# A mixture-of-experts layer step: gathered rows on three of every four partitions, half of the down product in f16 halves, SwiGLU clamps on the activation engine, weights split two units at once

## The chip, the cores and the metric

The kernel runs on one core of a Trainium2 chip. The metric is device time in microseconds (us) of one execution. Before the change the median of three runs is 1374.02 us (1372.73 to 1379.13). Five engines work side by side, each through its own list of instructions in order: TensorE (PE, with its weight loads PEld), VectorE (DVE), ScalarE (ACT), GpSimd (POOL) and SyncE (SP, which here only issues transfers). They wait for each other by semaphores alone. Sixteen DMA engines move data between the device memory, SBUF (128 partitions) and the tensors there.

## The reference

One inference step of a one-layer streaming encoder over 512 prompt rows and 64 sample rows of width 1024, all in f32:

```python
proj = x @ w_in -> [u | q | k | v | r | gate code]
A = multi-scale causal pooling mixer on u;  B = gated linear attention on q, k, v
h = LN1(alpha * x + concat(A, B) @ w_out)
y = LN2(alpha * h + MoE(h))            # and new pool and attention states

# MoE: top 4 of 32 experts by softmax router; each expert on its own rows xb
gu = xb @ w_gu[e] + b_gu[e]                              # 1024 -> 2 x 1024
gate, up = gu[:, :1024], gu[:, 1024:]
gate = minimum(gate, 7.0);  up = clip(up, -7.0, 7.0)
hmid = gate * sigmoid(1.702 * gate) * (up + 1.0)
out = hmid @ w_down[e] + b_down[e]                       # 1024 -> 1024
y_row = sum over the row's 4 experts of softmax weight * out
```

Each expert has 12 MB of f32 weights, 32 experts 403 MB. An expert has 72 rows on average.

## The kernel before, in words

The stage before the experts (projections, pooling, attention, first norm, router) takes about the first 285 us and is hardly touched. Then 32 experts follow, each in a block of 96 row places; experts with more rows get further blocks in a loop behind the 32, which the inputs of these runs do not enter.

**Weights.** SP loads an expert in six pieces of 2 MB (four of `w_gu`, two of `w_down`) into a ring of eight slots of 4096 f32 per partition. It may load a piece once the piece that held the slot has been read: for `w_gu` once DVE has split it (semaphore `split_done`), for `w_down` once PE has read it (`down_read`).

**Split products.** The product with `w_gu` runs in f16 halves. A *unit* is a block of 128 output columns with its 8 blocks of the inner dimension: 128x1024 elements. ACT writes the high half `whi = f16(1024 w)` (`hi`, L782), DVE then the low half `wlo = f16(1024 w - whi)` (`lo`, L1531). An expert has 16 units: 0 to 3 gate and 4 to 7 up of the first half of the hidden vector, 8 to 15 the same of the second half. There are 8 buffers for split units, so a unit can be split only when PE has used the unit eight before (`unit_used`). Per unit PE runs 24 matmuls of 96 columns (`unit`, L854).

**Activation.** Per half, DVE adds the bias, clamps and multiplies in seven instructions of 128x384 (`act_half`, L1501 to L1516), with the sigmoid on ACT between (L787). The result `hm` is the hidden vector, in f32.

**Down product.** PE multiplies `hm` by `w_down` in f32 straight from the ring (`down`): 16 products of 96x512, each of which is shown as two matmuls.

**Rows.** POOL gathers the rows of an expert two experts ahead with an indirect DMA into `xg`, 96 partitions (L582); the places come from a small product of one-hot `hot` with `info` (`table`, `rows_of`). PE transposes them (`rows`, L1098), ACT and DVE split them (`rows_hi` L774, `rows_lo` L1522). The output is weighed by ACT (L796) and scattered by POOL (L595).

**Order.** The order on every engine is written out by hand in its block. DVE, per expert: one-hot, lo of units 8 to 13, `act_half` 0, `rows_of`, lo 14 and 15, `act_half` 1, `rows_lo`, lo of units 0 to 7 of the next expert. PE: units 0 to 7, table, units 8 to 15, transposes of the next rows, down. At the end the partial rows of the four top-k places are loaded (L463), added on DVE (L1612) and on PE, and normed.

## Time and profile before

| | us |
|---|---|
| median of three runs | 1374.02 |
| lowest, highest | 1372.73, 1379.13 |
| profiled execution, own time | 1378.18 |
| its span (first to last instruction) | 1376.4 |
| PE busy | 1294.2 (94%) |
| DVE busy | 1009.2 (73%) |
| ACT busy | 677.4 (49%) |
| mean granted TensorE clock | 0.974 of full speed |

A profile shows one execution. Busy times of engines overlap; a share is an average over stages with different limits. "idle before" in a row is the time the engine stood still ahead of the instruction, and behind the arrow stands what ended it. The mean duration of one matmul is longer than its distance to the next, because matmuls are pipelined. Slices are fortieths of the span, 34.4 us each. The line numbers are of the kernel before.

### The profile page before, as it was taken

To read this page: it belongs to the slowest core of one execution; us is meant where nothing else is said; L and a number is where in the kernel's file an instruction comes from. 1 tells how busy PE (TensorE), PEld (TensorE's weight loads), DVE (VectorE), ACT (ScalarE), POOL (GpSimd) and SP (SyncE) were. 2 spreads that over 40 slices of the span, in tenths; PEclk is the share of its full clock that TensorE was granted. 3 is DMA by queue.
4 is the path that set the end of the run, shared out by engine and by line. 5 is a ranking of instruction groups with operands and counts; after the bars stand their busy time and mean duration, and the time that the engine had idled before them with its cause. 6 is when DMAs were issued, how large, how long until landed. Compare 5 with 4: busy or idle time off the path is not lost.

```text
span 1376.4 us, 34739 instructions
## 1 busy us (share of the span) xinstructions
PE 1294.2 (94%) x15208; PEld 885.9 (64%) x15208; DVE 1009.2 (73%) x1576; ACT 677.4 (49%) x814; POOL 121.9 (9%) x139
## 2 busy tenths in 40 slices
PE   6999989948999999999999999999999999999995
PEld 3446644446777777666666777777766666777652
DVE  4542436458888888788878788888878778787877
ACT  4531221044555655566655666555556556565611
POOL 1000811010100000000000000000000000000002
PEclk9999999959999999999999999999999999999997
DMA  9540155087999999999999999999999999999993
GB/s 323 210 181 1 55 192 214 16 315 281 398 401 409 413 411 412 414 413 409 400 407 414 410 412 409 412 414 414 417 409 404 407 411 410 410 413 414 390 389 101
DMA packets 50007, 472.62 MB, mean 343 GB/s; under 512 B 8542, under 2 KB 9333, under 8 KB 24637
## 3 DMA queue, kind: packets, MB, share of 16 engines
q1 hardware_dynamic: 38860, 436.22, 78.0%
q0 software_dynamic: 10336, 31.77, 6.4%
q8 instruction: 122, 2.00, 0.6%
q10 hardware_dynamic: 656, 2.36, 0.5%
q14 instruction: 33, 0.26, 0.1%
HBM read 446.43 MB, written 29.95 MB: 346 GB/s over the span
## 4 chain that ended last, share of the span: by engine, by line
PE 62%; DMA 10%; DVE 5%; issue 2%; ACT 1%; DVEq 0%; POOLq 0%
PE wide L854 45%; PE bank L854 16%; DMA ring<-in_w_gu 7%; DMA work<-part_rows 2%; DVE work L1531 2%; PE bank L1098 2%; ACT work L782 1%; DMA work<-h_rows,work 1%; DVE ring L1639 0%; DVE ring L1637 0%; DVE ring L1626 0%; DVE work L1501 0%; DVE work L1457 0%; DVE work L1504 0%; DVE ring L1373 0%
## 5 line engine op out<-in xcount | busy, mean ns | idle before, releaser
L1531 DVE SCALAR_TENSOR_TENSOR work<-ring,work 128x1024 f16<-128x1024 f32 x512 | 591.4, 1219 | 126.7 <-ACT work L782 126.3
L854 PE MATMUL wide<-ring,work 128*96 128x512 f32 (+4 forms) x1400 | 567.6, 564 | 1.8 <-ACT work L719 1.0
L782 ACT ACTIVATE work<-ring 128x1024 f16<-128x1024 f32 x512 | 500.8, 1048 | 80.6 <-DMA ring<-in_w_gu 68.2
L854 PEld LDWEIGHTS wide<-ring,work 128*96 128x96 f32 (+4 forms) x1400 | 215.2, 156 | 323.6 <-issue 299.1
L854 PE MATMUL wide<-work 128*128 128x96 f16 (+1 forms) x6262 | 304.5, 211 | 26.3 <-DVE work L1531 9.2
L854 PEld LDWEIGHTS bank<-work 128*128 128x128 f16 (+4 forms) x6450 | 296.0, 101 | 35.4 <-issue 23.4
L854 PE MATMUL bank<-work 128*128 128x96 f16 (+4 forms) x6450 | 301.8, 209 | 10.2 <-ACT work L755 3.8
L854 PEld LDWEIGHTS wide<-work 128*128 128x128 f16 (+1 forms) x6262 | 279.8, 99 | 46.6 <-issue 21.2
L787 ACT ACTIVATE work<-work 128x384 f32<-128x384 f32 x64 | 33.5, 524 | 199.8 <-DVE work L1504 199.8
L796 ACT ACTIVATE work<-wide,work 96x1024 f32<-96x1024 f32 x30 | 33.2, 1107 | 115.8 <-PE wide L854 115.7
L582 POOL DMA_INDIRECT work<-h_rows,work x32 | 31.8, 995 | 502.8 <-PE bank L1098 476.3
L595 POOL DMA_INDIRECT part_rows<-work x30 | 28.1, 938 | 426.2 <-ACT work L796 426.2
L774 ACT ACTIVATE work<-bank 128x384 f16<-128x384 f32 x64 | 28.2, 488 | 45.9 <-PE bank L1098 45.6
L1506 DVE SCALAR_TENSOR_TENSOR work<-wide,work 128x384 f32<-128x384 f32 x32 | 17.8, 557 | 41.5 <-PE wide L854 41.5
L1098 PE MATMUL bank<-work 96*128 96x96 f32 x256 | 28.5, 256 | 12.6 <-DMA work<-h_rows,work 12.1
L1522 DVE SCALAR_TENSOR_TENSOR work<-bank,work 128x384 f16<-128x384 f32 x64 | 32.6, 550 | 9.6 <-ACT work L774 9.5
L1416 DVE SCALAR_TENSOR_TENSOR ring<-ring,wide 128x1024 f32<-128x1024 f32 (+1 forms) x5 | 6.1, 1219 | 44.7 <-PE wide L854 44.7
L854 PE MATMUL wide<-work,ring 128*128 128x512 f16 (+2 forms) x296 | 38.7, 289 | 0.0
L1516 DVE TENSOR_TENSOR work<-work 128x384 f32<-128x384 f32 x64 | 35.9, 561 | 2.2
L1513 DVE SCALAR_TENSOR_TENSOR work<-work 128x384 f32<-128x384 f32 x64 | 35.8, 559 | 2.2
L1245 DVE SCALAR_TENSOR_TENSOR ring<-ring 128x1024 f16<-128x1024 f32 x16 | 19.0, 1222 | 20.4 <-ACT ring L670 20.4
L1098 PEld LDWEIGHTS bank<-work 96*128 96x128 f32 x256 | 23.7, 146 | 12.8 <-DMA work<-h_rows,work 12.2
(191 smaller groups left out, 609.8 us busy)
## 6 DMA issues: line engine op xcount, KB each, us to landing
ring<-in_w_gu SPq DMA_DIRECT2D x128, 2048.0 KB
ring<-in_w_down SPq DMA_DIRECT2D x64, 2048.0 KB
part_rows<-work POOLq DMA_DIRECT2D x1, 10240.0 KB, 37.1
ring<-in_w_in SPq DMA_DIRECT2D x4, 2048.0 KB
ring<-part_rows SPq DMA_DIRECT2D x3, 2560.0 KB, 26.3
ring<-in_w_out SPq DMA_DIRECT2D x2, 2048.0 KB
h_rows<-work POOLq DMA_DIRECT2D x1, 2560.0 KB, 9.9
ring<-h_rows SPq DMA_DIRECT2D x1, 2560.0 KB, 20.9
```

Of the source, the lines that this page charges most:

```text
L582: pool.indirect_dma_start(xg, None, h_dram, bass.IndirectOffsetOnAxis(ap=tok_i[q], axis=0), bounds_check=PLACES - 1, oob_is_err=False)\
L595: pool.indirect_dma_start(part_dram, bass.IndirectOffsetOnAxis(ap=dst_i[p], axis=0), orow, None, bounds_check=TOPK * SPAN - 1, oob_is_err= ...
L774: act.activation(xhi[q][:, 4 * b:4 * b + 4, :], bank[b][:, 0:4 * BLK] .rearrange("p (k s) -> p k s", k=4), ACT.Copy, scale=X_UP).then_inc( ...
L782: act.activation(whi[u % BUFS], packed(s, u), ACT.Copy, scale=W_UP).then_inc(hi_done, 1)
L787: act.activation(sg, g1, ACT.Sigmoid, scale=SWISH).then_inc(sig_done, 1)
L796: act.activation(orow, wide[1 if isinstance(n, int) else 0][0:BLK, :], ACT.Copy, scale=slots[p][:, 5:6])\
L854: return pe.matmul(out, w, x, start=start, stop=stop, skip_group_check=True)
L1098: last = pe.transpose(bank[b][:, k * BLK:(k + 1) * BLK], xg[:, (4 * b + k) * P:(4 * b + k + 1) * P], ident[0:BLK, 0:BLK])
L1513: dve.scalar_tensor_tensor(u1, u1, 1.0, g1, ALU.add, ALU.mult).then_inc(gate_up, 1)
L1516: dve.tensor_tensor(hm[:, 4 * half:4 * half + 4, :], u1, sg, ALU.mult).then_inc(hm_done, 1)
L1522: dve.scalar_tensor_tensor(xlo[q][:, 4 * b:4 * b + 4, :], bank[b][:, 0:4 * BLK] .rearrange("p (k s) -> p k s", k=4), X_UP, xhi[q][:, 4 * b ...
L1531: dve.scalar_tensor_tensor(wlo[u % BUFS], packed(s, u), W_UP, whi[u % BUFS], ALU.mult, ALU.subtract).then_inc(split_done, 1)
```

## The change

Five edits:

1. The one-hot has 128 columns instead of 96. Places 3, 7, 11, ... stay empty (`iota16`, which DVE fills in about a dozen small steps ahead of the first one-hot, is -1 there), so the 96 places lie on three of every four of 128 partitions, and `xg` has 128 partitions. The transpose multiplies by `used`, a permutation that brings the 96 used partitions to the front. A small product with `used16` (`sel_ready`) brings destinations and weights into the same order, and `places_of` reads them.
2. ACT and DVE split two units at once: 128x2048 elements in 4 buffers instead of 128x1024 in 8.
3. The first four of the eight inner blocks of the down product run in f16 halves: the first `w_down` piece is split as two more pairs (10 an expert, not 8), the hidden half too (`hidden_hi` on ACT, `hidden_lo` on DVE).
4. The clamps become Relu on ACT: `from_limit` writes relu(7 - (g + b)), scaled, once per 96 columns, since its bias is per output column: four instructions a quarter. A second Relu bounds `up` from the other side. DVE keeps two instructions per half, `gated_half` and `hidden`.
5. Nine matmuls that compute nothing stand ahead of the first rows (`idle`), the load of the second expert's first piece waits for the first gather, and the one-hots of the last stage are made after the last expert's units.

```diff
-BUFS = 8
+BUFS = 4
+PAIRS = 10
@@ SP, per expert
-                    if i < 2:
-                        sp.wait_ge(down_read, e * 2 + (i + 1))
+                    if e == 0:
...
+                    elif i == 1:
+                        sp.wait_ge(down_read, e + 1)
                     else:
-                        sp.wait_ge(split_done, e * 16 + 4 * (i - 1))
+                        sp.wait_ge(split_done, PAIRS * e - 2 if i == 0 else PAIRS * e + 2 * i - 4)
+                    if e == 1 and i == 0:
+                        sp.wait_ge(gathered[0], 16)
@@ SP, last stage
-                    sp.wait_ge(split_done, 16 * E + (4, 12, 16)[j])
+                    sp.wait_ge(split_done, PAIRS * E + (0, 4, 6)[j])
                 else:
-                    sp.wait_ge(unit_used, unit_done(E - 1, 15))
+                    sp.wait_ge(unit_used, pair_done(E - 1, 8))
@@ ACT
+            def hi(n, p, s, got):
+                if p % 2 == 0:
+                    act.wait_ge(slot_in[s], got)
+                act.wait_ge(unit_used, pair_done(n, p) - BUFS)
+                act.activation(whi[buf(n, p)], packed(s, p), ACT.Copy, scale=W_UP).then_inc(hi_done, 1)
+            def from_limit(dst, b, at):
+                for c in range(4):
+                    last = act.activation(dst[:, c, :], b[:, c * BLK:(c + 1) * BLK], ACT.Relu, scale=-DOWN * S_UP,
+                                          bias=bguT[:, at[0], at[1] + c:at[1] + c + 1])
+                return last
+            def gate(n, half, e):
+                act.wait_ge(unit_used, pair_done(n, 4 * half + 1))
+                act.wait_ge(hm_done, n * 2 + (half + 2))
+                from_limit(g1, bank[2] if half == 0 else wide[0][:, 0:512], (e, 4 * half)).then_inc(gate_free, 1)
+                act.wait_ge(gate_free, n * 2 + (half + 3))
+                act.activation(sg, g1, ACT.Sigmoid, scale=-SWISH / S_UP, bias=sig_bias).then_inc(sig_done, 1)
+            def up(n, half, e):
...
+                act.activation(u1, u1, ACT.Relu, scale=-1.0, bias=up_bias).then_inc(up_clip, 1)
+            def hidden_hi(n):
+                act.wait_ge(hm_done, n * 2 + 3)
+                act.wait_ge(unit_used, pair_done(n - 1, 9))
+                act.activation(hh, hm[:, 0:4, :], ACT.Copy, scale=1.0 / S_UP).then_inc(hh_done, 1)
             for n in range(E):
-                for u in range(BUFS, 16):
-                    if u == 14:
-                        swish(n, 0)
-                    hi(n, u, piece_slot(n, u // 4), landed(n, u // 4))
-                swish(n, 1)
+                next_hi(n, 4)
+                next_hi(n, 5)
+                gate(n, 0, n)
+                next_hi(n, 6)
+                next_hi(n, 7)
+                up(n, 0, n)
+                next_hi(n, 8)
+                hidden_hi(n)
+                next_hi(n, 9)
+                gate(n, 1, n)
+                if n + 1 < E:
+                    next_hi(n + 1, 0)
+                    next_hi(n + 1, 1)
+                up(n, 1, n)
...
@@ PE
-                    for k in range(4):
-                        last = pe.transpose(bank[b][:, k * BLK:(k + 1) * BLK],
-                                            xg[:, (4 * b + k) * P:(4 * b + k + 1) * P],
-                                            ident[0:BLK, 0:BLK])
+                        last = pe.transpose(bank[b][:, k * BLK:k * BLK + P],
+                                            xg[:, (4 * b + k) * P:(4 * b + k + 1) * P], used)
@@ def down(n, s, got)
+                    pe.wait_ge(hl_done, n + 1)
+                    for k in range(4):
+                        pe.wait_ge(split_done, pairs(n) + (8 + k // 2 + 1 + 2 * BUFS))
...
+                        for x, w in ((hh, wh), (hh, wl), (hl, wh)):
+                            for c in range(2):
+                                last = mm(out[:, c * 512:(c + 1) * 512], x[:, k, :], w[:, c * 512:(c + 1) * 512],
+                                          k == 0 and x is hh and w is wh, False)
+                        if k % 2:
+                            last.then_inc(unit_used, 1)
+                first = 4 if isinstance(n, int) else 0
+                for k in range(first, KT):
                     if k % 4 == 0:
                         pe.wait_ge(hm_done, n * 2 + (k // 4 + 3))
+            def idle(count):
+                for _ in range(count):
+                    mm(wide[1][:, 512:1024], ident, oT[:, 0, 0:512], True, True)
+            idle(3)
             table(0, 0)
+            idle(6)
             rows(0, 0, 16, 1)
@@ DVE
+            step(dve.memset(iota16, -1.0))
...
+            def gated_half(n, half):
+                dve.wait_ge(sig_done, n * 2 + (half + 1))
+                dve.scalar_tensor_tensor(g1, g1, -LIMIT * S_UP, sg, ALU.add, ALU.mult).then_inc(gated, 1)
+            def hidden(n, half):
+                dve.wait_ge(gated, n * 2 + (half + 1))
+                dve.wait_ge(up_clip, n * 2 + (half + 1))
...
+                dve.scalar_tensor_tensor(hm[:, 4 * half:4 * half + 4, :], u1, (1.0 - LIMIT) * S_UP, g1, ALU.add, ALU.mult)\
+                   .then_inc(hm_done, 1)
+            def lo(n, p, s):
+                dve.wait_ge(hi_done, pairs(n) + (p + 1))
+                dve.wait_ge(unit_used, pair_done(n, p) - BUFS)
+                dve.scalar_tensor_tensor(wlo[buf(n, p)], packed(s, p), W_UP, whi[buf(n, p)],
                                          ALU.mult, ALU.subtract).then_inc(split_done, 1)
```

How the order on DVE moves shows best in its list. Before, from the last two splits of an expert on (L1531 is a lo, L1501 to L1516 are `act_half` 1, L1522 is `rows_lo`, L1457 the one-hot):

```order
L1531 SCALAR_TENSOR_TENSOR work<-ring,work 128x1024 x2
L1501 SCALAR_TENSOR_TENSOR work<-wide,work 128x384
L1504 TENSOR_SCALAR work<-work 128x384
L1506 SCALAR_TENSOR_TENSOR work<-wide,work 128x384
L1509 TENSOR_SCALAR work<-work 128x384
L1513 SCALAR_TENSOR_TENSOR work<-work 128x384
L1516 TENSOR_TENSOR work<-work 128x384
L1522 SCALAR_TENSOR_TENSOR work<-bank,work 128x384 x2
L1531 SCALAR_TENSOR_TENSOR work<-ring,work 128x1024 x8
```

After, from the pair 8 split on (L1623 is a lo of a pair, L1608 `hidden_lo`, L1594 `gated_half` 1, L1603 `hidden` 1, L1614 `rows_lo`):

```order
L1623 SCALAR_TENSOR_TENSOR work<-ring,work 128x2048
L1608 SCALAR_TENSOR_TENSOR work<-work 128x384
L1623 SCALAR_TENSOR_TENSOR work<-ring,work 128x2048
L1594 SCALAR_TENSOR_TENSOR work<-work 128x384
L1623 SCALAR_TENSOR_TENSOR work<-ring,work 128x2048 x2
L1603 SCALAR_TENSOR_TENSOR work<-work 128x384
L1614 SCALAR_TENSOR_TENSOR work<-bank,work 128x384 x2
```

Two splits of the next expert now stand between `gated_half` 1 and `hidden` 1; before, every split of the next expert stood behind the finished hidden vector.

On PE, one expert before (L1098 are the transposes):

```order
L854 MATMUL bank<-work 128x96 x192
L854 MATMUL bank<-work 96x4 x5
L854 MATMUL wide<-work 128x96 x192
L1098 MATMUL bank<-work 128x96 x8
L854 MATMUL wide<-ring,work 96x512 x16
```

and after:

```order
L918 MATMUL bank<-work 128x96 x192
L918 MATMUL bank<-work 128x4 x5
L918 MATMUL wide<-work 128x96 x192
L918 MATMUL bank<-work 96x4
L1167 MATMUL bank<-work 128x128 x8
L918 MATMUL wide<-work 96x512 x24
L918 MATMUL wide<-ring,work 96x512 x8
```

Eight of the sixteen f32 products of the down product became 24 f16 ones, ahead of the eight that stay f32; those eight wait for `hidden` 1.

## Rows read from the trace of the kernel before

**Rows 1.** The page's 40 slices: busy share of the DMA engines in tenths.
```profile
DMA  9540155087999999999999999999999999999993
```
**Rows 2.** Chain of waits: start us, us, engine, line, count; expert starts and down products.
```profile
342.80 3.40 PE bank L854 x72
...
456.56 13.73 PE wide L854 x32
...
629.93 8.43 PE bank L854 x197
...
1058.63 13.75 PE wide L854 x32
...
1286.61 13.74 PE wide L854 x32
1300.35 8.16 PE bank L854 x192
```
**Rows 3.** Waits of ACT for weights, first in 456:1058, then in 1060:1290.
```profile
ACT work L782 <- DMA ring<-in_w_gu: 13.5, 9, 2.9
...
ACT work L782 <- DMA ring<-in_w_gu: 50.0, 20, 5.1
```
**Rows 4.** Windows: us, busy of PE, PEld, DVE, ACT, POOL, PEclk, DMA share, GB/s.
```profile
622.00:624.00 2.00, 2.00 (x6) 0.81 (x5) 2.00 (x3) 2.00 (x3) 0.00 (x0) 1.00 1.03 326
...
634.00:636.00 2.00, 2.00 (x52) 2.00 (x49) 2.00 (x3) 2.00 (x3) 0.00 (x0) 1.00 1.03 434
```
**Rows 5.** Timeline of one expert, 616:650.
```profile
617.04 0.96 POOL L582 DMA_INDIRECT work<-h_rows,work  x1 [15.92 <-PE bank L1098]
...
618.54 9.16 DVE L1531 SCALAR_TENSOR_TENSOR work<-ring,work 128x1024 f16<-128x1024 f32 x8
...
633.35 3.90 ACT L782 ACTIVATE work<-ring 128x1024 f16<-128x1024 f32 x4 [0.28 <-PE bank L854]
...
647.19 0.84 PE L1098 MATMUL bank<-work 96*128 96x96 f32 x8
```
**Rows 6.** Groups by line and form: busy us, mean ns of one, idle before.
```profile
L782 ACT ACTIVATE work<-ring 128x1024 f16<-128x1024 f32 x512 | 500.8, 1048 | 80.6 <-DMA ring<-in_w_gu 68.2 <-PE bank L854 12.2
L787 ACT ACTIVATE work<-work 128x384 f32<-128x384 f32 x64 | 33.5, 524 | 199.8 <-DVE work L1504 199.8
...
L719 ACT ACTIVATE work<-bank,work 128x64 f32<-128x64 f32 x4 | 1.2, 306 | 0.0
...
L1531 DVE SCALAR_TENSOR_TENSOR work<-ring,work 128x1024 f16<-128x1024 f32 x512 | 591.4, 1219 | 126.7 <-ACT work L782 126.3
...
L1513 DVE SCALAR_TENSOR_TENSOR work<-work 128x384 f32<-128x384 f32 x64 | 35.8, 559 | 2.2
```
**Rows 7.** Timelines: gaps of PE late in the stage; then a window of its clock.
```profile
1120.97 3.81 PE L854 MATMUL wide<-work 128*128 128x96 f16 x48 [2.12 <-DVE work L1531]
...
1283.60 2.33 PE L854 MATMUL wide<-work 128*128 128x96 f16 x48 [1.68 <-DVE work L1531]
...
1122.00:1123.00 1.00, 1.00 (x16) 0.50 1.00 426
```
**Rows 8.** Timeline of the first expert's start.
```profile
287.78 1.54 POOL L582 DMA_INDIRECT work<-h_rows,work  x1 [5.32 <-DVE work L1470]
...
298.60 1.54 PE L1098 MATMUL bank<-work 96*128 96x96 f32 x8 [12.10 <-DMA work<-h_rows,work]
...
324.42 2.98 PE L854 MATMUL wide<-work 128*128 128x96 f16 x48 [3.37 <-DVE work L1531]
```
**Rows 9.** Timeline of the last stage, 1320:1352.
```profile
1336.57 4.49 PE L854 MATMUL bank<-work 128*116 128x512 f16 x20
1340.90 5.49 DVE L1612 TENSOR_TENSOR ring<-ring 116x5120 f32<-116x5120 f32 x1 [0.64 <-DMA ring<-part_rows]
1346.94 17.22 PE L854 MATMUL wide<-work 116*116 116x512 f32 x44 [5.89 <-DMA work<-part_rows]
...
1350.81 1.23 DVE L1626 SCALAR_TENSOR_TENSOR ring<-wide,ring 116x1024 f32<-116x1024 f32 x1 [4.41 <-PE wide L854]
```

More of the change, by code:

```diff
@@ L230, in build @@
         val_one = take(E * (MAXB - 1))
+        hot30 = half_at(cursor[0], PLACES)
+        take(PLACES // 2)
+        hh, hl = [h[:, 0:4 * BLK].rearrange("p (k s) -> p k s", k=4) for h in (hot30, hot31)]
+        used16 = half_at(A + PLACES + 528 + D, BLK)
+        assert PLACES + 528 + D + BLK // 2 <= 2304
+        sig_bias, up_bias = small[:, 88:89], small[:, 89:90]
         g2n, b2n = ring[:, 0:D], ring[:, D:2 * D]
@@ L1455, in onehot @@
                     place = rank[0:n, t, bass.ds(e, 1)] if first is None else small[0:n, 59 + t:60 + t]
-                    order = places_b if isinstance(m, int) and m % 2 else iota16
-                    last = dve.tensor_scalar(hot[0:n, t, :], order[0:n, :], place, 1.0 / W_UP,
-                                             ALU.is_equal, ALU.mult)
+                    last = dve.tensor_scalar(hot[0:n, t, :], iota16[0:n, :], place, None, ALU.is_equal)
                 last.then_inc(hot_ready, 1)
@@ L1565, in _ @@
                     dve.memset(gatesT, 0.0).then_inc(gatesT_zero, 1)
[L1566 to L1572 removed]
+                next_lo(n, 8)
+                hidden_lo(n)
+                next_lo(n, 9)
+                gated_half(n, 1)
+                if n + 1 < E:
+                    next_lo(n + 1, 0)
+                    next_lo(n + 1, 1)
+                hidden(n, 1)
                 if n + 1 < E:
                     rows_lo(n + 1, (n + 1) % 2)
[L1575 to L1576 removed]
+                    places_of(n + 1, (n + 1) % ROW_BUFS)
+                    next_lo(n + 1, 2)
+                    next_lo(n + 1, 3)
+            dve.wait_ge(unit_used, pair_done(E - 1, 9))
+            dve.wait_ge(tok_known, 1)
+            end_hot(0)
+            end_hot(1)
             dve.wait_ge(gates_hi, 1)
@@ L1604, in _ @@
                     rows_lo(b + E, 0)
-                    for u in range(16):
-                        if u == 14:
-                            act_half(b + E, 0, e)
-                        lo(b + E, u, u // 4)
-                    act_half(b + E, 1, e)
+                    places_of(b + E, 0)
+                    dve.tensor_copy(bguT[:, E, :], bguT[:, bass.ds(e, 1), :].rearrange("p a f -> p (a f)"))\
+                       .then_inc(ov_bias, 1)
+                    for p in range(6):
+                        lo(b + E, p, p // 2)
+                    gated_half(b + E, 0)
+                    for p in range(6, 8):
+                        lo(b + E, p, p // 2)
+                    hidden(b + E, 0)
+                    gated_half(b + E, 1)
+                    hidden(b + E, 1)
             def add(j):
```

238 lines of the change are left out of this document (123 added, 115 removed).

## The prediction, written before the changed kernel was run

> **What bounds the kernel now.** I read the page's slices first: from the eleventh slice to the last but one the DMA engines are at 9 tenths or more [rows 1], so weights and compute have to be told apart. The chain of waits does that. It names PE nearly everywhere: 13.73 us of down product, 8.43 us for the first 192 f16 matmuls and the table's 5, and so on, one expert behind the other [rows 2]. An expert's own PE work is 2 x 8.43 + 0.84 [rows 5] + 13.73 = 31.4 us. Its period is (1058.63 - 456.56) / 19 = 31.69 us in the middle, and (1286.61 - 1058.63) / 7 = 32.57 us near the end; from the second expert's start to the last one's it is (1300.35 - 342.80) / 30 = 31.92 us. So PE is the limit for two thirds of the stage. Then the weights are late: ACT waits 13.5 us for them in the 602 us of the middle, 50.0 us in the 230 us behind [rows 3].
>
> Why they become late shows in the windows. The gather is issued at 617.04; at 622 to 624 the engines are full (share 1.03) but move 326 GB/s, where with the same share they move 434 a few us later [rows 4]. The lack is about 100 GB/s for some 5 us an expert, 0.5 MB or 1.1 us of DMA time. The scatter, issued at 631.95, has no such dip. 
>
> **The change part by part.** *Gather over 128 partitions.* At best the 1.1 us of DMA time go, and with them the late weights: the period near the end could be the 31.69 of the middle, 7 x 0.88 = 6 us in all. At worst nothing changes. The transposes read 128 columns for 96: 0.84 x 128/96 = 1.1 us, +0.3 on PE.
>
> *Down product.* Eight f32 products go, 13.73 / 2 = 6.87 us. 24 f16 ones of 512 columns come, at 4.49 / 20 = 0.22 us [rows 9]: 5.4 us. PE saves 1.5 us an expert. Its own work is then 16.9 + 0.2 (table) + 1.1 + 5.4 + 6.87 = 30.4 us. By that sum alone the kernel gains 1.5 x 30 = 45 us. But PE has to be fed.
>
> *Splits and activation.* A split of 1024 elements takes 1.05 us on ACT and 1.22 us on DVE [rows 6]; back to back they start (3.90 - 1.05) / 3 = 0.95 us apart on ACT and (9.16 - 1.22) / 7 = 1.13 us apart on DVE [rows 5]. From 384 to 1024 elements the duration grows 0.82 ns an element on ACT (524 to 1048 ns) and 1.03 on DVE (559 to 1219) [rows 6]. So a pair takes 1.9 us on ACT, one every 1.8; 2.28 us on DVE, one every 2.2. DVE has ten of them, 22 us, four 384-wide ones and `hidden_lo` at 0.5, `rows_lo` 1.0, one-hot 0.9, small ones 0.8: 27.2 us. It has no slack for waits inside 30.4 us, and the order puts one there: with 4 pair buffers, pair 4 may be split only when PE has read pair 0 of this expert.
>
> I follow one expert from T, when PE starts its pair 0. PE reads a pair in 8.43 / 4 = 2.1 us; ACT sees the end of a read 0.3 us late (units 0 to 2 end at 629.93 + 3.16 = 633.09, ACT goes on at 633.35 [rows 5]).
> - ACT: pair 5 from T + 4.5 (pair 1 read), then the four Relus of `gate` 0. They are not in the trace at 96 columns; with a bias by pointer 64 columns take 0.31 us [rows 6]. Four take between 0.6 us (overlapped like the splits) and 1.4 us (not at all); I take 1.0. Sigmoid 0.5, then hi of pair 6: 4.5 + 1.8 + 1.0 + 0.5 + 1.9 = T + 9.7.
> - DVE from there, without a pause: lo of pairs 6, 7, 8, 9 and of the next expert's 0 and 1, 6 x 2.2 = 13.2; between them `hidden` 0, `hidden_lo`, `gated_half` 1 at 0.5 and the table's copies 0.3; last `hidden` 1, 0.6: T + 25.6, with ACT just ahead of it on every pair.
> - PE needs `hidden` 1 for the f32 half. It is through with the f16 half at T + 16.9 + 0.2 + 1.1 + 5.4 = T + 23.6, and waits 2.0 us.
> - f32 half, 6.87: the next expert starts at T + 32.4.
>
> Behind `hidden` 1 DVE has `rows_lo`, `places_of`, two los and a one-hot, about 7 us, which just fit beside the f32 half. The period is 32.4 us for 31.92, +0.5 x 30 = +14 us. DMA needs less (12.6 MB of weights and 2 x 72 rows of 4 KB, 13.2 MB, at 434 GB/s: 30.4 us), so what the gather gives back is not on the path. In numbers the Relus move the period from 32.0 to 32.8. The Trainium skill (ScalarE: Activation LUTs, Rules for kernel authors) budgets about 0.3 us an ACTIVATE with such a bias plus 0.83 ns an element, and sends relu to VectorE. By that estimate four take 1.5 us and the period is 32.9; this trace has no row of four such in a row.
>
> *The clock.* The rows of before have two such gaps of PE amid dense work [rows 7]: 2.12 us, after which PE ran at 0.50, 1.2 GHz, in the window shown and its next 48 matmuls took 3.81 us, and 1.68 us, after which 48 matmuls took 2.33 us. The fall cost 1.5 us. My gap of 2.0 us stands between them, nearer the first. I take a fall after every second one: 15 x 1.5 = 22 us. Both ends, none and 30 (45 us), are for the range.
>
> *First expert.* The gather leaves later by about ten small DVE steps, 2 us, but lands sooner, since the load of the second expert's first piece now waits for it instead of going ahead of it: before, 10.8 us from issue to the transposes [rows 8]. PE's wait of 3.37 us for DVE [rows 8] comes in another form, and this expert loses 1.5 us of PE and the half clock at its start through the idle products. From 298.60 to 342.80 it took 44 us. Bounds 0 and -10, I take -7 us.
>
> *Last stage.* The last expert has no splits of a next one ahead of `hidden` 1, so no wait: -1.5 us. PE waits 5.89 us there for the last partial rows, which the lagging engines deliver at 1346.94 [rows 9]; if they lag less, DVE's third addition (ends 1346.4) is next, itself waiting for rows. Bounds 0 and -10, I take -6 us.
>
> **The sum.** 1376.4 + 14 + 22 - 7 - 6 = 1399.4 us of span, with the 1.8 around it 1401.2. The profiled execution is 4.2 above the median, so 1397 us as a median.
>
> **The rivals.**
> - *The wait without the clock.* Same period, the clock holds as after 1.68 us: 1397 - 22 = 1375 us, no change. For it: one of two rows, and a gap 0.1 below the one that did fall. Against: it has to hold 30 times.
> - *The clock falls every time.* 1397 + 23 = 1420 us. The mechanism: a gap of 2.0 us at one place in every expert, its price 1.5 us, decided somewhere between 1.68 and 2.12 us of gap. [...]
> - *PE becomes the bound as the edit would have it.* ACT and DVE run ahead, `hidden` 1 is there at T + 23.6. Then the period is 30.4 and some tenths, say 31.0: 1374 - 13 - 30 x 0.92 = 1333 us, faster. It needs 2 us less on the chain above, Relus at their lower end and pair splits below my slope. For it: DVE's 27.2 us would fit if nothing waited. Against: no edit removes the wait for pair 1.
> - *The gather keeps its price.* If the slow packets come from something else than the partitions, the DMA's own period near the end stays at 32.57, hidden under 32.4 but for 0.2, and the last stage gains nothing: 1397 + 5 = 1402 us.
>
> **How the numbers follow.** A difference of 0.5% (7 us) is about what a measurement tells. Forecast 0.38, own range 1383 to 1412; clock holds 0.18; falls every time 0.12; PE the bound 0.22; gather keeps its price 0.10. Slower by over 0.5%: 0.38 + 0.12 + 0.10 less a little for shorter Relus, 0.58. Faster: 0.22 and a part of the second, 0.24. Within: 0.18. The range runs from 1345, half-way into the case in which PE is the bound, to 1425, just past the fall every time.
>
> **What would show it.** In the profile after: (1) windows under a gather at over 400 GB/s, ACT's wait for weights gone: the gather edit works; (2) PE in every expert idle about 2 us ahead of the f32 half, ended by the DVE line of `hidden`, period 32.4 or with a fall 34; (3) a granted clock under 0.97; (4) DVE never idle between the lo of pair 6 and `hidden` 1; (5) pair splits of 1.9 and 2.28 us. A period below 31.7, or PE waiting for something else, makes the prediction wrong; a pair on DVE of under 2.1 us makes its sum wrong.

## The result, and the profile after

The kernel before took 1373.72 us (1372.73 to 1379.13), the changed one 1387.69 us (1385.73 to 1395.49, 4 runs): a ratio of 1.0104, 95% interval 1.0056 to 1.0152, so about 1% slower. I had forecast slower, at 1397 us. The profiled execution of the changed kernel is its slowest (1395.49 us, span 1393.7 us, clock 0.973); the other three had clocks of 0.977 to 0.98. This profile holds some 8 us more than the median. Its clock is the lowest of the four, and each fall of the clock costs 1.7 us (below), so that 8 us would be about five falls; the other three executions have no profile that could show it.

From the page after: the busy shares, and the DMA slices that answer to [rows 1].

```profile
PE 1272.4 (91%) x15514; PEld 904.3 (65%) x15514; DVE 1040.4 (75%) x1205; ACT 939.4 (67%) x1230; POOL 143.5 (10%) x139
...
DMA  9640254098999999999999999999999999999892
...
ACT 31%; PE 28%; issue 11%; DVE 9%; DMA 0%; POOL 0%; DVEq 0%; ACTq 0%; POOLq 0%
```

The last line is the chain's share by engine: it now runs over ACT more than over PE. The chain's own pieces answer to [rows 2] (start, us, engine, line, count):

```profile
336.02 4.09 PE bank L918 x96
...
593.83 7.11 PE wide L918 x16
...
626.13 7.11 PE wide L918 x16
...
658.44 8.80 PE wide L918 x16
...
1318.09 7.11 PE wide L918 x16
1325.20 4.09 PE bank L918 x96
```

From one f32 half of the down product to the next, 593.83 to 626.13 to 658.44, it is 32.30 us, and most periods of the trace are that to 0.01 us. The half at 658.44 takes 8.80 us instead of 7.11, and the period that begins with it is 34.00. From the second expert's start (336.02, before 342.80) to the last one's (1325.20) it is 32.97 us on average, before 31.92. The rest of the span is 1393.7 - 1325.2 = 68.5 us, before 76.0. So: -6.8 us up to the second expert, +31.6 us over 30 periods, -7.5 us behind, together the +17.3 us between the two spans.

One expert in the timeline of the changed kernel, from one f32 half to the next (start, us, engine, line, operation, tiles, count, and in brackets the idle time before and what ended it). It answers to [rows 5].

```profile
626.13 7.11 PE L918 MATMUL wide<-ring,work 128*96 128x512 f32 x16 [2.17 <-DVE work L1603]
...
633.08 8.51 PE L918 MATMUL bank<-work 128*128 128x96 f16 x197
...
637.32 4.49 DVE L1623 SCALAR_TENSOR_TENSOR work<-ring,work 128x2048 f16<-128x2048 f32 x2 [4.64 <-PE bank L918]
639.17 1.01 ACT L812 ACTIVATE work<-bank,work 128x96 f32<-128x96 f32 x4
...
650.99 5.37 PE L918 MATMUL wide<-work 128*96 128x512 f16 x24
651.49 3.69 ACT L807 ACTIVATE work<-ring 128x2048 f16<-128x2048 f32 x2
...
653.42 4.49 DVE L1623 SCALAR_TENSOR_TENSOR work<-ring,work 128x2048 f16<-128x2048 f32 x2
655.09 1.01 ACT L812 ACTIVATE work<-wide,work 128x96 f32<-128x96 f32 x4
656.14 0.62 ACT L828 ACTIVATE work<-work 128x384 f32<-128x384 f32 x1
...
657.83 0.55 DVE L1603 SCALAR_TENSOR_TENSOR work<-work 128x384 f32<-128x384 f32 x1
...
658.44 8.80 PE L918 MATMUL wide<-ring,work 128*96 128x512 f32 x16 [2.08 <-DVE work L1603]
```

L1603 is `hidden`. At 650.99 PE begins the f16 half, is through at 656.36, and waits for `hidden` 1, which ends at 658.4. Ahead of it DVE has the two splits for the next expert (653.42, 4.49 us), and ACT the four Relus and the clip of `up` 1 (655.09 to 656.76). Over 456 to 1290 the waits of PE for it add up (waits: engine, what for, us in total, times, longest). That is 1.8 us on average, but they are not alike: the period stays at 32.30 us while the wait runs from 0.8 to 2.35 us, because in many experts PE has lost a part of it before, in the f16 work (see the last section).

```profile
PE wide L918 <- DVE work L1603: 46.0, 26, 2.4
```

ACT's wait for weights [rows 3] is gone. Before, the slow windows began 5 us behind the issue of the gather (617.04 us, windows from 622 on). Here the gather is issued at 619.58 us, and the windows that answer to [rows 4] show no slow one; the 397 GB/s stand beside a DMA share of 0.93, which was 1.03 at 326 GB/s:

```profile
622.00:624.00 2.00, 1.96 (x9) 0.87 (x7) 2.00 (x2) 1.97 (x6) 0.00 (x0) 1.00 1.08 451
624.00:626.00 2.00, 0.00 (x0) 0.00 (x0) 2.00 (x3) 2.00 (x4) 0.00 (x0) 1.00 0.93 397
626.00:628.00 2.00, 1.87 (x5) 0.81 (x6) 1.97 (x8) 2.00 (x2) 0.00 (x0) 1.00 1.04 440
```

The mean over the 26 gathers between 450 and 1290 us says the same: from 5 to 8 us behind the issue the engines moved 322 GB/s before, and 427 in the changed kernel.

The clock, in windows of 1 us around the second gap above (busy of PE, PEld, DVE, ACT, POOL, then the granted clock, the DMA share, GB/s), against [rows 7]:

```profile
657.00:658.00 1.00, 0.00 (x0) 0.00 (x0) 1.00 (x2) 1.00 (x3) 0.00 (x0) 1.00 0.97 410
658.00:659.00 1.00, 0.56 (x1) 0.24 (x2) 1.00 (x3) 1.00 (x1) 0.00 (x0) 0.88 1.22 516
659.00:660.00 1.00, 1.00 (x3) 0.32 (x2) 0.97 (x6) 1.00 (x2) 0.00 (x0) 0.50 0.72 303
```

From 658.8 to 662.2 it is at 0.50, 1.2 GHz, just behind PE's gap. Such falls stand at ten places of the profile between 456 and 1290 us, each 3.4 us long and 1.7 us dear (34.00 - 32.30); before there was one. And the groups by line and form that answer to [rows 6]:

```profile
L1623 DVE SCALAR_TENSOR_TENSOR work<-ring,work 128x2048 f16<-128x2048 f32 x320 | 721.7, 2288 | 180.3 <-PE bank L918 164.1 <-ACT work L807 11.8 <-issue 0.3
L807 ACT ACTIVATE work<-ring 128x2048 f16<-128x2048 f32 x320 | 598.6, 1900 | 38.6 <-PE bank L918 36.4
...
L812 ACT ACTIVATE work<-bank,work 128x96 f32<-128x96 f32 x256 | 64.8, 333 | 0.0
```

At the two ends, the first expert's transposes and the chain's additions of the last stage, against [rows 8] and [rows 9]:

```profile
292.25 1.10 PE L1167 MATMUL bank<-work 128*128 128x128 f32 x8 [2.10 <-DMA work<-h_rows,work]
```

```profile
1351.42 5.50 DVE ring L1724
```

The transposes start 6.35 us sooner. The change did only 2.4 us of that. The last top-8 search of the router (MAX8 on DVE), ahead of the gather and of the experts, starts at 280.31 us in the profile before and at 276.38 us in this one, and in the profiles of the twelve experiments, whose work up to there is the same, anywhere from 276.24 to 280.47 us. So 3.9 us of the 6.8 are scatter of the stage ahead of the experts.

In the last stage PE no longer waits 5.89 us for partial rows; DVE's additions set the pace. The rows' load now lands sooner (from the page: KB each, us from issue to landing; before, then after):

```profile
ring<-part_rows SPq DMA_DIRECT2D x3, 2560.0 KB, 26.3
...
ring<-part_rows SPq DMA_DIRECT2D x3, 2560.0 KB, 13.8
```

### The profile page after: what moved, and what is told of

Its sections match the earlier page's. It is cut to its first block, busy times and chain, and to the rows that moved or that the text cites. A ratio compares the mean times of both kernels' runs of the same rounds, so it can differ in the third digit from the quotient of the medians.

```text
span 1393.7 us, 35273 instructions
## 1 busy us (share of the span) xinstructions
PE 1272.4 (91%) x15514; PEld 904.3 (65%) x15514; DVE 1040.4 (75%) x1205; ACT 939.4 (67%) x1230; POOL 143.5 (10%) x139
## 3 DMA queue, kind: packets, MB, share of 16 engines
q0 software_dynamic: 11360, 31.77, 6.0%
## 4 chain that ended last, share of the span: by engine, by line
ACT 31%; PE 28%; issue 11%; DVE 9%; DMA 0%; POOL 0%; DVEq 0%; ACTq 0%; POOLq 0%
ACT work L807 21%; PE wide L918 18%; PE bank L918 10%; ACT work L812 8%; DVE work L1623 4%; ACT work L828 2%; DVE work L1603 1%; DVE ring L1724 1%; ACT work L833 1%; DVE ring L1751 0%; DMA work<-h_rows,work 0%; DVE ring L1749 0%; DVE ring L1738 0%; DVE work L1532 0%; POOL work L647 0%
## 5 line engine op out<-in xcount | busy, mean ns | idle before, releaser
L1623 DVE SCALAR_TENSOR_TENSOR work<-ring,work 128x2048 f16<-128x2048 f32 x320 | 721.7, 2288 | 180.3 <-PE bank L918 164.1
L807 ACT ACTIVATE work<-ring 128x2048 f16<-128x2048 f32 x320 | 598.6, 1900 | 38.6 <-PE bank L918 36.4
L918 PE MATMUL wide<-work 128*128 128x96 f16 (+3 forms) x7048 | 479.4, 229 | 23.1 <-issue 14.8
L918 PEld LDWEIGHTS wide<-work 128*128 128x128 f16 (+3 forms) x7048 | 373.5, 101 | 111.9 <-issue 33.8
L918 PE MATMUL wide<-ring,work 128*96 128x512 f32 (+4 forms) x888 | 365.8, 570 | 54.6 <-DVE work L1603 53.6
L918 PEld LDWEIGHTS bank<-work 128*128 128x128 f16 (+2 forms) x6482 | 297.7, 101 | 36.0 <-issue 24.3
L918 PE MATMUL bank<-work 128*128 128x96 f16 (+3 forms) x6482 | 305.7, 208 | 9.0 <-ACT work L780 3.8
L918 PEld LDWEIGHTS wide<-ring,work 128*96 128x96 f32 (+4 forms) x888 | 136.0, 157 | 266.2 <-issue 173.9
L812 ACT ACTIVATE work<-bank,work 128x96 f32<-128x96 f32 x256 | 64.8, 333 | 0.0
L812 ACT ACTIVATE work<-wide,work 128x96 f32<-128x96 f32 x256 | 64.7, 330 | 0.0
L828 ACT ACTIVATE work<-work 128x384 f32<-128x384 f32 x64 | 39.4, 616 | 2.1
L1501 DVE SCALAR_TENSOR_TENSOR ring<-ring,wide 128x1024 f32<-128x1024 f32 (+1 forms) x5 | 6.1, 1219 | 41.3 <-PE wide L918 41.3
L1603 DVE SCALAR_TENSOR_TENSOR work<-work 128x384 f32<-128x384 f32 x64 | 35.4, 552 | 0.2 <-DVE work L1594 0.2
L1594 DVE SCALAR_TENSOR_TENSOR work<-work 128x384 f32<-128x384 f32 x64 | 35.4, 553 | 0.0
L1614 DVE SCALAR_TENSOR_TENSOR work<-bank,work 128x384 f16<-128x384 f32 x64 | 32.4, 548 | 3.3 <-ACT work L799 3.3
```

The lines of the kernel that those rows point to most:

```text
L807: act.activation(whi[buf(n, p)], packed(s, p), ACT.Copy, scale=W_UP).then_inc(hi_done, 1)
L812: last = act.activation(dst[:, c, :], b[:, c * BLK:(c + 1) * BLK], ACT.Relu, scale=-DOWN * S_UP, bias=bguT[:, at[0], at[1] + c:at[1] + c + 1])
L828: act.activation(u1, u1, ACT.Relu, scale=-1.0, bias=up_bias).then_inc(up_clip, 1)
L918: return pe.matmul(out, w, x, start=start, stop=stop, skip_group_check=True)
L1594: dve.scalar_tensor_tensor(g1, g1, -LIMIT * S_UP, sg, ALU.add, ALU.mult).then_inc(gated, 1)
L1603: dve.scalar_tensor_tensor(hm[:, 4 * half:4 * half + 4, :], u1, (1.0 - LIMIT) * S_UP, g1, ALU.add, ALU.mult)\
```

## The experiments

The theory: the period is a chain, from PE's read of pair 1 over ACT's `gate` 0 and pair 6 and over six splits on DVE to `hidden` 1; PE's saved 1.5 us an expert come back as a wait ahead of the f32 half, and some of these waits let the clock fall. The rivals: DVE's load as such is the limit; the gather still costs what it did; the gap costs nothing by itself and only the clock does. The runs are the changed kernel with one edit, 5 and 6 with that of experiment 1 and one or two more; the kernel before was timed beside them in three groups (1 to 4, 5 to 8, 9 to 12; medians 1375.3, 1374.24 and 1375.34 us).

**1 and 2. `hidden` 1 ahead of the next expert's splits** (the calls of both engines side by side, shortened).

```
 DVE:  gated_half(n, 1)            ACT:  gate(n, 1, n)
+      hidden(n, 1)               +      up(n, 1, n)
       next_lo(n + 1, 0)                 next_hi(n + 1, 0)
       next_lo(n + 1, 1)                 next_hi(n + 1, 1)
-      hidden(n, 1)               -      up(n, 1, n)
```

> The changed kernel with one move: hidden 1 (DVE) and up 1 (ACT) stand ahead of the two splits of the next expert. Theory (PE waits about 2.1 us in every expert because these two splits stand ahead of hidden 1): the wait ahead of the f32 half goes, the clock no longer falls, the period falls from 32.97 us (32.3 without falls) to PE's own 30.4 to 31.0, span 1394 - 30 x 2.0 to 2.5 = 1320 to 1335 us. Rival (the period is set by the total work of DVE and ACT, or by the loads at 30.4 to 31.7 us an expert): the wait only moves to another place, the time stays above 1360 us.

> The changed kernel with hidden 1 ahead of the two splits on DVE alone; on ACT up 1 stays behind the two hi. Theory: hidden 1 then waits for up 1, which ACT ends at T + 24.0; PE's wait shrinks from 2.1 to about 0.6 us, no clock falls, period 30.9 to 31.1 us, 5 to 15 us slower than with both moved. Rival (DVE's order alone mattered): same time as with both moved.

Both moved: 1335.42 us, ratio to before 0.9706 (0.9675 to 0.9736). DVE alone: 1343.88 us, ratio 0.9779 (0.9751 to 0.9807). The timeline with both moved, one expert:

```profile
623.26 5.38 PE L918 MATMUL wide<-work 128*96 128x512 f16 x24
...
625.87 0.56 DVE L1603 SCALAR_TENSOR_TENSOR work<-work 128x384 f32<-128x384 f32 x1
...
628.48 7.03 PE L918 MATMUL wide<-ring,work 128*96 128x512 f32 x16
```

`hidden` 1 is there 2 us before the f16 half ends, and PE goes on without a gap. With DVE's part alone the same place reads:

```profile
637.96 0.61 ACT L828 ACTIVATE work<-work 128x384 f32<-128x384 f32 x1
...
638.66 0.56 DVE L1603 SCALAR_TENSOR_TENSOR work<-work 128x384 f32<-128x384 f32 x1 [3.57 <-issue]
...
639.28 3.25 PE L918 MATMUL wide<-ring,work 128*96 128x512 f32 x7 [1.24 <-DVE work L1603]
```

Now DVE stands idle 3.57 us. The view names nothing that ended it ("issue"), but `hidden` 1 waits for ACT's clip of `up` 1 (L828), and that ends at 638.57, 0.09 us ahead of it: ACT's half of the chain is 1.0 us shorter than DVE's was, and the period is 31.32 us, 0.98 less, where I had expected 30.9 to 31.1. The gap is 1.24 us here and nowhere over 1.4, and the clock does not fall between 330 and 1310 us. The wait is shown, and so is the second limit 1 us below it. With both moved, windows and waits between 456 and 1290 name the third:

```profile
456.00:1290.00 834.00, 809.58 (x11768) 619.97 (x11765) 727.06 (x739) 716.39 (x915) 89.65 (x51) 1.00 1.01 424
...
ACT work L807 <- DMA ring<-in_w_gu: 60.6, 45, 3.9
```

PE's own period is 29.71 us (seen from 605.80 to 635.51 to 665.22); from the second expert's start (331.42) to the last one's (1256.68) it is 30.84 on average, with ACT waiting for weights at 424 GB/s. DMA is the limit again, and this version is the fastest measured here. Its last stage takes 76.7 us, as long as before (76.0) and not the 68.5 of the changed kernel.

**3. The gap filled.** Twelve products of 96 x 384 that nobody reads, between the f16 and the f32 half:

```
+                if isinstance(n, int) and n + 1 < E:
+                    pe.wait_ge(gate_free, n * 2 + 3)
+                    for _ in range(12):
+                        mm(bank[2][0:BLK, 0:4 * BLK], xhi[n % 2][:, 0, :], hh, True, True)
```

> The changed kernel with 12 matmuls of 384 columns that compute nothing on PE between the f16 and the f32 half of every down product but the last, 1.9 us. Theory of the clock (a PE gap of about 2.1 us makes the clock fall after some experts, 1.7 us each, ten times in the profile after): PE goes on waiting for hidden 1, the period is 32.3 in every expert, the clock 0.99, the median 10 to 17 us below the changed kernel's: 1371 to 1378 us. Rival (falls come from elsewhere, or the dummies push the f32 half back): no gain or a loss of up to 0.5 us an expert.

1386.32 us (1379.87 to 1389.97), ratio 1.0077 (1.0055 to 1.01): hardly less than the changed kernel, and above the 1371 to 1378 that I had expected. Its profile (span 1380.8 us) has no fall of the clock between 340 and 1320 us, where the changed kernel's has ten. But the filling takes the whole wait, and here more than that:

```profile
620.68 2.11 PE L918 MATMUL bank<-work 128*96 128x384 f16 x12
620.70 0.55 DVE L1607 SCALAR_TENSOR_TENSOR work<-work 128x384 f32<-128x384 f32 x1
...
622.64 7.03 PE L918 MATMUL wide<-ring,work 128*96 128x512 f32 x16
```

`hidden` 1 (here L1607) is done at 621.25 and the f32 half starts at 622.64, behind the last idle product. In this expert PE had lost 1.12 us in its f16 work before ("issue", ahead of 610.49), and there is no wait left in which such a loss could vanish. From 360.86 to 1303.64 the mean period is 32.51 us, 0.21 more than the chain needs: 6 us given back, 17 saved, 11 in all of the 12.9 us between the two spans. In the medians only 1.4 us of it are seen: the profiled execution of the changed kernel was slower than its median and this one faster than its own (1382.54 us). By the medians it stays open how much the filling is worth.

**4 and 11. The gather as it was.** First the rows back on partitions 0 to 95, the gather still issued over 128; then issued over 96 as well:

```
-            from_rank = iota1[:, 0:BLK].rearrange("p (d x a c e) -> p d x a c e", d=3, x=2, a=2, c=4)
...
+            step(dve.tensor_copy(used, ident))
+            by_rank = iota1[:, 0:BLK].rearrange("p (k a) -> p a k", a=16)
+            step(dve.tensor_copy(iota16[:, 0:BLK].rearrange("p (a k) -> p a k", a=16), by_rank))
```

and in 11 alone

```
-                pool.indirect_dma_start(xg, None, h_dram,
-                                        bass.IndirectOffsetOnAxis(ap=tok_i[q], axis=0),
+                pool.indirect_dma_start(xg[0:BLK, :], None, h_dram,
+                                        bass.IndirectOffsetOnAxis(ap=tok_i[q][0:BLK, :], axis=0),
```

> The changed kernel with the gathered rows on partitions 0 to 95 of the 128 again (the permutation is the identity). Theory (packed partitions slow the gather and the weights beside it, but the loads are not the limit at a period of 32.3): under a gather the rate falls to about 330 GB/s again, the time is within 0.5% of the changed kernel's, with up to 7 us more in the last stage, where the engines lag. Rival (the partitions are not what slowed them): no dip. Rival (the spread is what keeps the changed kernel at this period): over 10 us slower.

> The changed kernel with the gather as before: rows on partitions 0 to 95, issued over 96. Where DMA was the limit this issue cost 24.5 us over the packed rows alone, 0.85 us an expert, a period of 31.99 us. Here the period is 32.30 us, so DMA has 0.3 us to spare even so: 1387 us as with the packed rows, to 1392 if the last stage's rows come later as in my rival (its +5 us). If the price is paid here too: 1387 + 25 = 1412 us.

1387.43 us, ratio 1.0086 (1.0053 to 1.0118), and 1388.65 us, ratio 1.0123 (1.0068 to 1.0178). Both are the changed kernel's time: its way of gathering brought nothing to it. In the first the slow windows that my theory of the packed rows had expected did not come (427 GB/s from 5 to 8 us behind the issue, as the mean of 26 gathers), so that theory is out. In the second they are back (336 GB/s, and 332 in the next 2 us; 328 in the same mean) all the same, under a gather issued at 620.67 us:

```profile
626.00:628.00 2.00, 0.53 (x2) 0.26 (x3) 2.00 (x4) 2.00 (x3) 0.00 (x0) 1.00 1.04 336
```

Nothing waits for them: the period without a fall stays at 32.31 us, and its last stage takes 68.6 us, where the changed kernel's takes 68.5.

**5 and 6. The same two edits where DMA is the limit**, on top of experiment 1.

> The version with hidden 1 moved ahead on both engines (1335.4 us, 424 GB/s in its middle, ACT waits for weights 60.6 us between 456 and 1290), and in it the gathered rows on partitions 0 to 95 in a row, while the gather is still issued over 128 partitions. Here DMA is the limit, so that a price of the gather shows in the time. If packed rows are what slowed the weights before (1.1 us of DMA time an expert by my prediction): 1335 + 30 x 1.1 = 1366 us, and windows under the gather at about 330 GB/s. If it was the issue over 96 partitions, and not where the rows lie: 1335, or up to 1342 because 12 of the 16 engines then carry all rows, and no slow window.

> As the run with packed rows, and the gather issued over 96 partitions only, as in the kernel before. Both theories of the gather (the partitions of the rows, the count of partitions of the issue) expect its whole price here: 1335 + 33 = 1366 us, windows of about 330 GB/s under the gather. If the slow windows of before came from something else that has changed with it (the state of the queue, which was always behind there), it stays at 1335 to 1342.

1345.77 us, ratio 0.9777 (0.975 to 0.9805), and 1370.3 us, ratio 0.997 (0.9955 to 0.9985). Windows under a gather, first with packed rows issued over 128 partitions, then with the same rows issued over 96:

```profile
666.00:668.00 2.00, 2.00 (x6) 0.81 (x5) 2.00 (x2) 2.00 (x2) 0.00 (x0) 1.00 1.02 430
668.00:670.00 2.00, 2.00 (x6) 0.76 (x5) 1.97 (x7) 1.60 (x1) 0.00 (x0) 1.00 1.04 434
```

```profile
668.00:670.00 2.00, 2.00 (x6) 0.68 (x5) 1.38 (x1) 2.00 (x2) 0.00 (x0) 1.00 1.04 342
670.00:672.00 2.00, 2.00 (x6) 0.79 (x5) 2.00 (x2) 1.14 (x3) 0.00 (x0) 1.00 1.03 311
```

So it is the count of partitions in the issue that makes the weights slow, not where the rows lie: 24.5 us, or 0.8 us an expert. Where they lie is worth another 10.4 us (1335.42 to 1345.77), 3.8 us more than the 1342 that I had allowed for it. In the two profiles 4.4 of 11.7 us stand ahead of the second expert, where one profile differs from another by such amounts anyway, and 7.2 us, 0.24 an expert, in the 30 periods behind. The cause is open; there is no slow window under the packed rows. The Trainium skill (DMA: Bandwidth & Descriptors, The descriptor swizzle) gives a formula by which, in a transfer over 128 partitions, engines 0 to 7 write partitions 0 to 63 and engines 8 to 15 the rest. By it, packed rows put eight rows on each of the first eight engines and four on the others, spread rows six on each, which would fit; no row here tells the engines apart. By the same formula all sixteen engines carry packed rows, and not twelve, as I had written ahead of experiment 5; no run shows either.

**7 and 8. One more operation on DVE**, 0.68 us long, ahead of `hidden` 1 (7), or behind the last split before the wait for pair 4 (8).

```
                 if n + 1 < E:
                     next_lo(n + 1, 0)
                     next_lo(n + 1, 1)
+                step(dve.tensor_reduce(small[:, 90:91], work[:, 0:512], AX.X, ALU.add))
                 hidden(n, 1)
```

```
                     next_lo(n + 1, 3)
+                step(dve.tensor_reduce(small[:, 90:91], work[:, 0:512], AX.X, ALU.add))
```

> The changed kernel with one more operation on DVE (a sum over 512 columns into a free column, estimated 0.55 to 0.7 us) directly ahead of hidden 1. If the chain over DVE from the wait for pair 1 to hidden 1 sets the period, all of it comes on top: 32.30 + 0.6 = 32.9 to 33.0 us, +18 to +21 us, PE's gap 2.7 to 2.9 us. If a gap makes the clock fall the more surely the longer it is, the clock now falls in nearly all 30 experts instead of 10, +30 us more: 1387 + 20 + 30 = 1437 us; if falls don't hang on the length of this gap, 1408 us. If DVE's waits take it up (DVE is idle 4.6 us an expert ahead of pair 4): 1387 us.

> The changed kernel with the same additional operation on DVE, but behind the last split ahead of the wait for pair 4, where DVE is idle 4.6 us in every expert. If only the chain from that wait on counts, it costs nothing: 1384 to 1390 us, period 32.30, and DVE's wait is shorter by its duration. If DVE's total load is what sets the period: 1387 + 20 = 1407 us.

1431.31 us, ratio 1.0391 (1.0356 to 1.0426), and 1389.61 us, ratio 1.0089 (1.0058 to 1.012). The same 0.68 us cost 44 us in one place and nothing in the other. In the first:

```profile
637.58 0.68 DVE L1673 TENSOR_REDUCE work<-work 128x1 f32<-128x512 f32 x1
638.29 0.56 DVE L1603 SCALAR_TENSOR_TENSOR work<-work 128x384 f32<-128x384 f32 x1
...
638.90 8.80 PE L918 MATMUL wide<-ring,work 128*96 128x512 f32 x16 [2.97 <-DVE work L1603]
```

Its period without a fall is 33.03 us, 0.73 more, which is the operation and its start: 22 us. The other half is the clock: 20 falls between 340 and 1370 us instead of 10, three of them 7 us long. It went by what I expected of the chain and of the clock (1437 us), a little less.

**9. One Relu for four in `gate` 0.** It leaves out that each 96 columns have a bias of their own.

```
+                if half == 0 and isinstance(n, int):
+                    act.activation(g1, bank[2][:, 0:4 * BLK].rearrange("p (k s) -> p k s", k=4), ACT.Relu,
+                                   scale=-DOWN * S_UP, bias=bguT[:, e, 0:1]).then_inc(gate_free, 1)
...
```

> The changed kernel with gate's first half in one Relu over 384 columns instead of four over 96; it leaves out that each block of 96 has its own bias (all four take the first one's). 0.62 us for 1.01. If the chain from pair 1's read over gate 0, pair 6 and the six splits behind it to hidden 1 sets the period, all 0.39 us come off: 32.30 - 0.39 = 31.9 us, -12 us in all, and PE's gap shrinks to about 1.7 us; in the traces so far the clock fell after none of 35 gaps of up to 1.75 us and after 42 of 80 longer ones, so that the falls should go as well, -15 us: about 1361 us. If ACT isn't on that chain: 1387 us.

1370.51 us (1365.64 to 1377.81, 10 runs), ratio 0.9971 (0.9947 to 0.9995). The operation (groups by form) takes 0.56 us where four took 1.01:

```profile
L820 ACT ACTIVATE work<-bank,work 128x384 f32<-128x384 f32 x32 | 18.0, 564 | 0.0
```

The period without a fall is 31.86 us, 0.45 less, the whole difference; so ACT's `gate` 0 is on the chain. Of the rest I expected too much. Where PE loses nothing on the way, its gap in the changed kernel was 2.35 us and not 2.1, and here gaps of 1.97 to 2.12 us are left in several experts. The clock still fell four times between 340 and 1320 us in the profile, each time behind a gap of 1.99 to 2.12 us, and the ten runs have clocks from 0.976 to 0.985, the slowest run with the second lowest of them. The median came 9.5 us above my number.

**10. ACT's part of the move alone.**

```
                 gate(n, 1, n)
+                up(n, 1, n)
                 if n + 1 < E:
                     next_hi(n + 1, 0)
                     next_hi(n + 1, 1)
-                up(n, 1, n)
```

> The changed kernel with only ACT's part of the move: up 1 ahead of the next expert's first two splits; DVE keeps hidden 1 behind its two. In the trace of the changed kernel DVE starts the next expert's lo 0 within 0.2 us of ACT's hi 0, so ACT has no slack there. By the chain this order makes it worse: hi 0 leaves 1.6 us later (four Relus 1.0, the clip 0.6), hidden 1 as well, period 33.9 us, +48 us, gap 3.7 us, and most gaps let the clock fall, +25 us: about 1460 us. If it is the number of splits ahead of hidden 1 on either engine that counts, and not this chain, it is at 1387 us or below.

1460.66 us, ratio 1.0616 (1.058 to 1.0652), where the chain had said 1460.

```profile
675.79 4.50 DVE L1623 SCALAR_TENSOR_TENSOR work<-ring,work 128x2048 f16<-128x2048 f32 x2 [1.71 <-ACT work L807]
...
680.20 0.55 DVE L1603 SCALAR_TENSOR_TENSOR work<-work 128x384 f32<-128x384 f32 x1
680.81 8.57 PE L918 MATMUL wide<-ring,work 128*96 128x512 f32 x16 [3.25 <-DVE work L1603]
```

DVE waits 1.71 us for ACT ahead of the two splits, and the period is 33.87 us, 1.57 more. The half of an edit that gains 52 us costs 73 by itself: no count of operations gives that, only the order of the waits.

**12. No idle products ahead of the first expert.**

```
-            idle(3)
             table(0, 0)
-            idle(6)
             rows(0, 0, 16, 1)
```

> The changed kernel without the nine idle products on PE ahead of the first expert. They take 5.4 us in which PE would wait for the gathered rows anyway. If they keep the clock up for the first expert, it starts at 1.2 GHz without them and the second expert's start moves from 336.0 us to 338 or 339; in the total +2 to +3 us, under what the comparison can tell, so that the profile decides. If DVE sets the pace there anyway, nothing moves.

1394.21 us (1387.75 to 1398.45), ratio 1.0157 (1.0123 to 1.0191). In the profile the first expert's f32 half starts at 327.59 us against 327.21: the idle products are worth 0.4 us there. The median is 6.5 us above the changed kernel's and its interval overlaps; the profiled execution of 1387.75 us has five falls of the clock, the other three runs have lower clocks (0.967 to 0.972, it 0.974). That the idle products do more than the profile shows is open.

## Why the prediction was right, point by point

*What bounds the kernel.* Right in the kernel before. The gather does slow the weights, and 1.1 us of DMA time an expert holds: the traffic that a gather displaces in the profile before is 0.46 MB, 1.1 us at 425 GB/s. In the time of the kernel 0.8 us of it are seen, by experiments 5 and 6. Where I put it was wrong: the remedy is the issue over 128 partitions, which came with the spreading, more than the spreading itself. Of the Trainium skill's rules that I had weighed, the one on a transfer over 128 partitions, which gives each engine one port (DMA: Bandwidth & Descriptors, The descriptor swizzle), is the half that agrees, with 430 GB/s for 311; the ports themselves no row shows.

*The chain.* With T = 633.08, ACT's pair 6 ends at 642.6, T + 9.6 (predicted 9.7), PE's f16 half at 656.36, T + 23.3 (23.6), `hidden` 1 at 658.4, T + 25.3 (25.6); the next expert starts at T + 32.3 (32.4) where the clock holds, and at T + 34.0 behind this one, where it fell. The 25.6 and what follows from it hold an error: the terms that stand there, 9.7 + 13.2 + 1.5 + 0.3 + 0.6, add up to T + 25.3. By that sum the wait is 1.7 us, the period 32.2 and its share of the forecast +7 us, not +14; the measured 25.3 agrees with the terms, and the +11 us lies between the two. PE's own part was 0.3 us shorter than my 23.6, too, and the two errors cancel in the wait: 2.0 us forecast, 2.08 measured here. That is luck, and the clock term hangs on it: beside my rows a wait of 1.7 us would have stood with the 1.68 that held, not with the 2.12 that fell. Four Relus take 1.01 us for 1.0, pairs 1.90 and 2.29 us for 1.9 and 2.28. The Trainium skill's budget for the Relus (ScalarE: Activation LUTs, Rules for kernel authors), by which I had estimated 1.5 us, is too high by half for four in a row: they take 0.33 us each, but start 0.23 us apart. Experiments 7, 9 and 10 add and take away time on this chain and give them back within 0.05 us. One step was incomplete: ACT was "just ahead of it on every pair", but its own `up` 1 ends only 1.0 us before DVE is ready for `hidden` 1. It would have shown that moving DVE's part alone shortens the period by 1 us and not by 2.

*Period.* 32.30 for 31.92, times 30: +11 us, predicted +14. *Clock.* "After every second one: 15 x 1.5 = 22 us"; measured ten times 1.7 = 17 us, in the execution in which the clock was lowest. In an execution at the median, 7.8 us faster, I estimate 9 us from the same price, so that this term was more than twice too large there. The sign (3), a clock under 0.97, did not come: it was 0.973 to 0.98. The remaining 3 us of the stage are longer periods at its start (33.7 us) and near 495 us. *First expert.* -6.8 for -7 is luck: 3.9 us of it are scatter ahead of the router's end (276.38 for 280.31 us), and what the change itself brought is -2.9 us. *Last stage.* -7.5 for -6, but the reason was wrong: I had it from the lagging engines of the gather, and with the gather issued as before (experiment 11) it is 68.6 us too. It went because the weights no longer queue. In the four profiles in which weights are late (before, experiments 1, 5 and 6) the partial rows land 26.3 to 27.5 us behind their issue and the last stage takes 76 to 78 us; in the other ten they land after 13.4 to 14.2 us, whatever the gather.

*The sum.* 1393.7 us of span for 1399.4. The median is 9 us under my 1397: 6 from the sum, the rest because I took the profiled execution as 4.2 above the median, and it was 7.8.

*The rivals.* "The clock holds" would have been 1375 us; the falls decide between it and what happened. "Falls every time" didn't happen: nearly the same gap in the same place (2.21 us at 923.64, 2.17 at 957.64) lets the clock fall in one expert and not in the next, and what decides is not shown. "PE becomes the bound" gave 1333 us and needed 2 us less on the chain: experiment 1 takes them away and measures 1335.4. That the numbers meet is in part luck: PE alone would need 29.71 us a period there, and the weights make it 30.84. "The gather keeps its price" (1402 us) is out: the price is 0 in this kernel by experiments 4 and 11.

## What to carry to other kernels

Where two engines prepare work for a third, lay the chain through all three from one fixed point, and ask of each operation ahead of the awaited one whether anyone needs it sooner: here the whole change turned from -38 us to +14 on two splits that stood ahead of one short product. Move such an operation on every engine of the chain or on none (+73 us for the wrong half, -44 and -52 for the right half and the whole). A saving on the engine that seems to be the limit is worth only what the next limit leaves, and a gap that it opens can cost more than its length through the clock.

## What the runs showed of the hardware

An indirect gather of the same 96 rows slowed the other transfers from about 430 to 311 to 342 GB/s when issued over 96 partitions, and not when issued over 128, 32 of which fetch nothing that is used. The page shows the 1024 more packets (32 gathers by 32) and no more bytes on that queue:

```profile
q0 software_dynamic: 11360, 31.77, 6.0%
```

with 10336 and 31.77 MB in the kernel before and in experiments 6 and 11. A longer list was the faster one.

The granted clock fell after some gaps and not after others of the same length. I counted PE's gaps ahead of the f32 half in eight profiles (the changed kernel and experiments 4 and 7 to 12, the second to the 30th expert) against the granted clock: after gaps of up to 1.75 us it fell 0 times of 91, from 1.75 to 2.4 us 39 of 97, above that up to 3.9 us 31 of 44. The shortest gap with a fall behind it is 1.94 us, the longest without one 3.49 us. A period that is too long is not always a fall: near 460 us one of 33.4 us stands in several of these profiles with the clock at full. A fall of 3.4 us costs 1.7 us. The times of one kernel scatter by 10 us, in step with the mean clock.

PE also loses 0.2 to 1.5 us in some experts inside the f16 part, marked "issue", 10.7 us in all between 456 and 1290 us in the changed kernel. With a wait behind it that costs nothing: the period is 32.30 us with it or without, and the wait is shorter by as much. Where the wait is filled (experiment 3) it does cost.
